# Weights in two longer rings, with a distance within 512 bytes for each kind of product

## What is computed

```python
def first_block(x, ...):          # DEPTH = 2
    for layer in range(DEPTH):
        y = rms_norm(h, nw[0])
        y = even_mixer(...) if layer % 2 == 0 else odd_mixer(...)   # attention + gated recurrence / attention with bias
        h = h + rms_norm(y, nw[1])
        y = conv_ffn(rms_norm(h, nw[2]), ffn_w_up[layer], ...)      # 1024 -> 2 x 2816, conv, 2816 -> 1024
        h = h + rms_norm(y, nw[3])

def second_block(x, mem, ...):    # one layer
    proj = rms_norm_2(x, g_mix) @ w_in      # q, k, v of three attentions, three gates
    merged = sum of sigmoid(gate) * (attention @ w_br)
    x = x + merged @ w_out
    x = x + (silu(h2 @ w_gate) * (h2 @ w_up)) @ w_down
```

## Time and profile before

| what | us |
|---|---|
| median of 3 runs | 1095.84 |
| lowest, highest | 1094.64, 1097.82 |
| profiled execution | 1095.88 |
| span in its profile | 1094.1 |
| PE busy | 1086.6 |
| DVE busy | 748.6 |
| ACT busy | 600.4 |
| POOL busy | 109.1 |

### The profile page before, as it was taken

One profiled execution on the slowest core, in us unless ns is written; L12 is line 12 of the kernel. 1 busy time (PEld: TensorE's weight loads), 2 busy tenths in 40 slices (PEclk: granted clock), 3 DMA queues, 4 the chain that ended last, 5 costly groups with the idle time before them and its releaser, 6 DMA issues.

```text
span 1094.1 us, 16723 instructions
## 1 busy us (share of the span) xinstructions
PE 1086.6 (99%) x6712; PEld 959.6 (88%) x6712; DVE 748.6 (68%) x1109; ACT 600.4 (55%) x994; POOL 109.1 (10%) x127
## 2 busy tenths in 40 slices
PE   8999999999999999999999999999999999999998
PEld 7988989888888899898888888889999989888887
DVE  7876595998846566859788566766656885666651
ACT  6744465776734545557667445357444644555640
POOL 4020000121100000001111001121000000111100
PEclk9999999999999999999999999999999999999999
DMA  8751356666664755366566656474433555666661
GB/s 287 284 174 59 121 206 211 193 190 188 185 192 152 269 150 146 126 225 189 187 190 184 195 182 212 135 234 135 115 99 113 167 159 196 189 181 187 192 193 39
DMA packets 56957, 192.29 MB, mean 176 GB/s; under 512 B 6832, under 2 KB 9776, under 8 KB 56880
## 3 DMA queue, kind: packets, MB, share of 16 engines
q1 hardware_dynamic: 56880, 191.22, 55.2%
HBM read 190.15 MB, written 1.05 MB: 175 GB/s over the span
## 4 chain that ended last, share of the span: by engine, by line
PE 95%; DVE 2%; POOL 1%; ACT 1%; issue 0%; DMA 0%; DVEq 0%; ACTq 0%; POOLq 0%
PE ps L929 28%; PE ps L1019 19%; PE ps L1010 15%; PE ps L1020 10%; PE ps L1285 5%; PE ps L1159 3%; PE ps L1105 3%; PE ps L1082 2%; PE ps L1346 2%; PE ps L1094 1%; PE ps L1031 1%; PE ps L1144 1%; DVE lo L1485 1%; POOL hr L533 1%; PE ps L1051 1%; PE ps L1169 1%
## 5 line engine op out<-in xcount | busy, mean ns | idle before, releaser
L1485 DVE TENSOR_TENSOR lo<-raw,hi 128x1024 fp32r<-128x1024 f32 (+2 forms) x347 | 429.1, 1263 | 81.9 <-ACT hi L588 79.1
L588 ACT ACTIVATE hi<-raw 128x1024 fp32r<-128x1024 f32 (+2 forms) x347 | 347.0, 1036 | 82.2 <-DMA raw<-in_weights 75.5
L1019 PE MATMUL ps<-y_both,hi 128*128 128x512 f32 x912 | 320.8, 397 | 0.0
L1020 PE MATMUL ps<-y_both,lo 128*128 128x256 f32 x912 | 255.0, 280 | 0.0
L1019 PEld LDWEIGHTS ps<-y_both,hi 128*128 128x128 f32 x912 | 171.3, 188 | 41.5
L1020 PEld LDWEIGHTS ps<-y_both,lo 128*128 128x128 f32 x912 | 171.9, 189 | 0.0
L1010 PE MATMUL ps<-y_both,hi 128*128 128x256 f32 x912 | 167.6, 285 | 0.3 <-DVE lo L1485 0.3
L1010 PEld LDWEIGHTS ps<-y_both,hi 128*128 128x128 f32 x912 | 141.8, 191 | 1.1 <-DVE lo L1485 0.5
L1010 PE MATMUL ps<-y_both,lo 128*128 128x256 f32 x456 | 128.9, 283 | 0.0
L929 PE MATMUL ps<-hi,y_both 128*128 128x512 f32 x352 | 94.1, 382 | 2.2 <-DVE lo L1485 1.4
L929 PE MATMUL ps<-hi,h_hi 128*128 128x512 f32 x294 | 90.9, 391 | 0.0
(11 more groups left out here) (291 smaller groups left out, 1386.2 us busy)
## 6 DMA issues: line engine op xcount, KB each, us to landing
raw<-in_weights SPq DMA_DIRECT2D x331, 512.0 KB, 3.7
gain<-in_gains SPq DMA_DIRECT2D x10, 512.0 KB, 7.2
raw<-in_weights SPq DMA_DIRECT2D x8, 384.0 KB, 7.2
bias<-in_rel SPq DMA_DIRECT2D x16, 128.0 KB, 2.1
raw<-in_weights SPq DMA_DIRECT2D x8, 256.0 KB, 2.6
mem_x<-in_mem SPq DMA_DIRECT2D x2, 512.0 KB, 9.8
h<-in_x SPq DMA_DIRECT2D x2, 256.0 KB, 2.7
h<-in_x SPq DMA_DIRECT2D x1, 512.0 KB, 6.1
```

Source lines behind the costliest of these rows:

```text
L588: act.activation(hi[:, s, :w], raw[:, s, :w], ACT.Copy).then_inc(hi_done, 1)
L1019: pe.matmul(dst, hi[:, s, at], y_both[:, :, k, :], start=k == 0, stop=False)
L1020: mm = pe.matmul(dst[:, 0:S], lo[:, s, at], y_hi[:, k, :], start=False, stop=k == KD - 1)
L1485: dve.tensor_tensor(lo[:, s, :w], raw[:, s, :w], hi[:, s, :w].bitcast(F32), ALU.subtract).then_inc(lo_done, 1)
```

## The change

The slots are replaced by two rings of single values. `lo` and `raw` get LO_RING = 10 x 1024 + 144 values, `hi` gets HI_RING = 10 x 1024 + 240. DIST gives for a kind two distances in steps of 64 bytes, of hi and of lo: how far, modulo 512 bytes, token slices lie behind weight slices. Feature-major kinds get (1, 7), leads and up get (1, 0), all others (0, 0). `ring()` places each unit in each ring behind the one before, moved up to the next place that has its distance, or at the front where the ring's end is reached; GIVER is the latest unit that lay on any part of either place. The load's semaphore goes by n modulo 10. To make room, block_causal moves into mk_t, snk and esnk into top and tot, warm is cut, and align goes. The places at the changes of kind, worked out from the code: units 8 to 14 and 16 to 22 have a giver 7 before them instead of 8; units 32 and 33 start in or reach into the kept region and have giver 31; units 34 to 39 have one 10 before them; 40 has giver 31 as before, 41 has 32 instead of 31 and 42 has 33 instead of 32; 84 to 92, 114 to 122, 130 to 132, 134 to 142, 182, 184 to 190, 237 to 242, 244, 245, 274 to 282 and 325 to 332 have one 9 before them instead of 10; all others keep 10.

```diff
+DIST = {"even_f": (1, 7), "even_q": (1, 7), "odd_qk": (1, 7), "gates": (1, 7), "branches": (1, 7),
+        "lead0": (1, 0), "lead1": (1, 0), "lead2": (1, 0), "up0": (1, 0), "up1": (1, 0), "up2": (1, 0)}
+STEP, LINE = 16, 128
+LO_RING, HI_RING = RAW * UNIT + LINE + STEP, RAW * UNIT + LINE + 7 * STEP
 def ring():
-    free = [(s, -1) for s in range(FEW)]
+    kept = (RAW - FEW) * UNIT
+    names = [name for name, n, _, _ in STREAM for _ in range(n)]
+    owner = [[-1] * HI_RING, [-1] * LO_RING]
+    end, at, giver = [0, 0], [], []
     for n in range(UNITS):
-        free.append((free[n][0], n))
-        if n == last("fill") - 1:
-            free += [(s, n) for s in range(FEW, RAW)]
-    slot, giver = [x[0] for x in free[:UNITS]], [x[1] for x in free[:UNITS]]
-    return slot, giver, [slot[:n + 1].count(slot[n]) for n in range(UNITS)]
+        both, last_owner = [], -1
+        for i, size in enumerate((HI_RING, LO_RING)):
+            if n < last("fill"):
+                size -= kept
+            elif n == last("fill"):
+                owner[i][size - kept:] = [n - 1] * kept
+            rest = STEP * ((7, 0)[i] - DIST.get(names[n], (0, 0))[i]) % LINE
+            p = end[i] + (rest - end[i]) % LINE
+            if p + UNIT > size:
+                p = rest
+            end[i] = p + UNIT
+            last_owner = max(last_owner, *owner[i][p:p + UNIT])
+            owner[i][p:p + UNIT] = [n] * UNIT
+            both.append(p)
+        at.append(both)
+        giver.append(last_owner)
+    return at, giver
...
-            lo = sb("lo", [RAW, UNIT], F32R, r)
-        raw = sb("raw", [RAW, UNIT])
-        hi = sb("hi", [RAW, UNIT], F32R)
+            lo = sb("lo", [LO_RING], F32R, r)
+        raw = sb("raw", [LO_RING])
+        hi = sb("hi", [HI_RING], F32R)
...
-        m_hi = lo[:, FEW:RAW, :].rearrange("p a (b s) -> p (a b) s", s=S)
-        m_lo = hi[:, FEW:RAW, :].rearrange("p a (b s) -> p (a b) s", s=S)
+        m_hi = lo[:, LO_RING - (RAW - FEW) * UNIT:].rearrange("p (k s) -> p k s", s=S)
+        m_lo = hi[:, HI_RING - (RAW - FEW) * UNIT:].rearrange("p (k s) -> p k s", s=S)
...
-                sp.dma_start(raw[:, SLOT[n], :WIDTH[n]], dram["weights"][n][:, :WIDTH[n]]).then_inc(raw_in[SLOT[n]], 16)
+                sp.dma_start(raw_at(n)[:, :WIDTH[n]], dram["weights"][n][:, :WIDTH[n]]).then_inc(raw_in[n % RAW], 16)
```

More of the change, by code:

```diff
@@ L227, in build @@
         mv = sb("mv", [NT, 512])
+        block_causal = mk_t[:, 0, 0:P].bitcast(U32)
         sc = sb("sc", [2, 512])
@@ L254, in build @@
         rec = sb("rec", [20, 2])
-        snk = sb("snk", [8, 2])
-        esnk = sb("esnk", [8, 2])
+        snk, esnk = top[:, 8:16, :], tot[:, 8:16, :]
         ncum = sb("ncum", [S])
@@ L471, in _ @@
                 (keep[:, :], dram["c_keep"]),
[L472 removed]
+                (window[:, :], dram["c_window"]), (block_causal, dram["c_block"]),
                 (hw[:, :], dram["hgrn_w"].partition_broadcast(P)),
@@ L778, in _ @@
                     act.activation(whole(hg), whole(hg), ACT.Silu).then_inc(hg_evac, 1)
-                    act.activation(warm[:, 8:16], half[:, 8:16], ACT.Exp)
+                    act.activation(warm[:, :], half[:, 8:16], ACT.Exp)
                 if hh in (4, 6):
@@ L785, in _ @@
             act.wait_ge(dve_sink, 1)
-            act.activation(esnk[:, :, :], snk[:, :, :], ACT.Exp).then_inc(act_sink, 1)
+            act.activation(esnk, snk, ACT.Exp).then_inc(act_sink, 1)
             even_hi(1, 1, 2)
@@ L888, in _ @@
             gate_copy(11)
-            act.activation(warm[:, 8:16], half[:, 8:16], ACT.Sigmoid)
+            act.activation(warm[:, :], half[:, 8:16], ACT.Sigmoid)
             for b in range(4):
@@ L1008, in features_of @@
                         at = slice(k * cols + f * P, k * cols + (f + 1) * P)
-                        for w, x, first, final in ((hi, yh, True, False), (hi, yl, False, False), (lo, yh, False, True)):
-                            mm = pe.matmul(dst, w[:, s, at], x(k), start=first and k == 0, stop=final and k == nk - 1)
+                        for w, x, first, final in ((hi_at, yh, True, False), (hi_at, yl, False, False), (lo_at, yh, False, True)):
+                            mm = pe.matmul(dst, w(n)[:, at], x(k), start=first and k == 0, stop=final and k == nk - 1)
                 return mm
             def features_pair(n, dst):
-                s = SLOT[n]
                 pe.wait_ge(lo_done, n + 1)
@@ L1018, in features_pair @@
                     at = slice(k * P, (k + 1) * P)
-                    pe.matmul(dst, hi[:, s, at], y_both[:, :, k, :], start=k == 0, stop=False)
-                    mm = pe.matmul(dst[:, 0:S], lo[:, s, at], y_hi[:, k, :], start=False, stop=k == KD - 1)
+                    pe.matmul(dst, hi_at(n)[:, at], y_both[:, :, k, :], start=k == 0, stop=False)
+                    mm = pe.matmul(dst[:, 0:S], lo_at(n)[:, at], y_hi[:, k, :], start=False, stop=k == KD - 1)
                 return mm
@@ L1142, in _ @@
                         k = 2 * (n - FIRST["even_i"]) + kk
-                        for x, w in ((y_hi, hi), (y_hi, lo), (y_lo, hi)):
-                            mm = pe.matmul(ps[:, 4 + t, :], x[:, k, t * P:(t + 1) * P], w[:, SLOT[n], 512 * kk:512 * kk + 512],
-                                           start=k == 0 and x is y_hi and w is hi, stop=k == KD - 1 and x is y_lo)
+                        for x, w in ((y_hi, hi_at), (y_hi, lo_at), (y_lo, hi_at)):
+                            mm = pe.matmul(ps[:, 4 + t, :], x[:, k, t * P:(t + 1) * P], w(n)[:, 512 * kk:512 * kk + 512],
+                                           start=k == 0 and x is y_hi and w is hi_at, stop=k == KD - 1 and x is y_lo)
                 mm.then_inc(unit_used, 1)
@@ L1157, in fill @@
                         wait_unit(n)
-                    for x, w in ((yh, hi), (yh, lo), (yl, hi)):
-                        mm = pe.matmul(ps[:, 6, t * 256:t * 256 + 256], x[:, k, t * P:(t + 1) * P], w[:, SLOT[n], c],
-                                       start=k == 0 and x is yh and w is hi, stop=k == KD - 1 and x is yl)
+                    for x, w in ((yh, hi_at), (yh, lo_at), (yl, hi_at)):
+                        mm = pe.matmul(ps[:, 6, t * 256:t * 256 + 256], x[:, k, t * P:(t + 1) * P], w(n)[:, c],
+                                       start=k == 0 and x is yh and w is hi_at, stop=k == KD - 1 and x is yl)
                     if t == 1 and k % 4 == 3:
@@ L1189, in even_part @@
                     wait_unit(n)
-                for x, w in ((y_hi, hi), (y_hi, lo), (y_lo, hi)):
+                for x, w in ((y_hi, hi_at), (y_hi, lo_at), (y_lo, hi_at)):
                     for c in range(2):
-                        mm = pe.matmul(ps[:, (0, 6)[t] + c, :], x[:, k, tok], w[:, SLOT[n], 512 * c:512 * c + 512],
-                                       start=u == 0 and x is y_hi and w is hi, stop=u == KD - 1 and x is y_lo)
+                        mm = pe.matmul(ps[:, (0, 6)[t] + c, :], x[:, k, tok], w(n)[:, 512 * c:512 * c + 512],
+                                       start=u == 0 and x is y_hi and w is hi_at, stop=u == KD - 1 and x is y_lo)
                 if t == 1:
@@ L1284, in lead @@
                                     k, c = 4 * half_ + kk, slice(256 * kk, 256 * kk + 256)
-                                    mm = pe.matmul(lead_place(layer, j, t), x[:, k, tok], w[:, SLOT[n], c],
+                                    mm = pe.matmul(lead_place(layer, j, t), x[:, k, tok], w(n)[:, c],
                                                    start=k == 0 and i == 0, stop=k == KD - 1 and i == 2)
@@ L1343, in out_part @@
                     wait_unit(n)
-                for x, w in ((0, hi), (0, lo), (1, hi)):
+                for x, w in ((0, hi_at), (0, lo_at), (1, hi_at)):
                     for c in range(2):
-                        mm = pe.matmul(ps[:, (6, 0)[t] + c, :], out_y(x, k // 4, tok)[:, k % 4, :], w[:, SLOT[n], 512 * c:512 * c + 512],
-                                       start=k == 0 and x == 0 and w is hi, stop=k == KD - 1 and x == 1)
+                        mm = pe.matmul(ps[:, (6, 0)[t] + c, :], out_y(x, k // 4, tok)[:, k % 4, :], w(n)[:, 512 * c:512 * c + 512],
+                                       start=k == 0 and x == 0 and w is hi_at, stop=k == KD - 1 and x == 1)
                 if t == 1:
```

55 lines of the change are left out of this document (30 added, 25 removed).

## The result

| what | before | after |
|---|---|---|
| median, runs timed together | 1096.83 us (1094.64 to 1098.11) | 1117.1 us (1116.52 to 1118.75) |
| span of the profiled execution | 1094.1 us | 1115.8 us |
| mean granted TensorE clock | 1.00 | 0.988 |

The changed kernel is slower by 1.9%: the ratio is 1.0187, with a 95% interval of 1.0169 to 1.0205. It is 20.3 us longer, where 8.9 us were predicted. The direction and the range held, and the size was half of what came. In the changed kernel the same lines have numbers higher by 28 or 29: L929 is now L958, L1010 is L1039, L1019 and L1020 are L1047 and L1048, L1285 is L1313, L1031 is L1059, L1192 is L1220, L1346 is L1374.

What follows compares the result with a forecast made beforehand. PE, busy for 99% of the span, was taken as the bound. 1095.9 us less 23.7 saved by quicker products plus 32.6 for waits and restarts gave 1104.8 us, range 1083 to 1128.

Steps and rivals of the forecast that it cites:

- The four stops: New PE waits around even_out and odd_out because loads get later givers: 28.6 us of cost, bounds 27 and 30.
- A: Going into even_out, units 32 and 33 wait for unit 31: PE idles 7.3 to 9.1 us, 8.3 taken.
- B: Leaving even_out, unit 42 waits for unit 33 and holds up the norms: 7.1 us of new PE wait.
- C: In odd_out, unit 139 waits for 130 and its hi holds up out_hi: PE waits 5.9 us at out_part(4, 0).
- D: Leaving odd_out, unit 140 waits for 131, the first of the second pass: 7.3 us of PE wait.
- the waits are covered after all: Rival: engines not held up by unit order, or quicker loads, leave about 10 us of cost: 1082 us, chance 0.08.
- Starting again: Behind each of four idle spells PE runs at half pace: 0 to 9.6 us of cost, 4 taken.
- Feature-major products: 1440 products in even_f, even_q, odd_qk, gates and branches go from 120 to 112 ns: 11.4 us saved.
- Pairs: 912 pairs of 512 and 256 columns in the up stages go to 339 ns each: 10.0 us saved.
- The start: At the kernel's start units 8 to 14 come one release later: costs nothing, 1.5 us at most.
- The distance takes all of it away: Rival: feature-major and lead products reach 109 ns, pairs 325: 43.4 us saved, 1085 us, chance 0.20.
- The distance does nothing: Rival: the excess is a fixed cost of switching weights, so nothing is saved: 1128.5 us, chance 0.17.

Runs made afterwards that it cites:

- e1: The kernel before, slots and addresses kept, but each load waits for the later of its own giver and the changed kernel's: 1133.65 us, ratio 1.0328.
- e2: The changed kernel, but the ring may use the kept region only from unit 40 on: 1099.41 us, ratio 1.0021.
- e3: e2 with odd_qk, even_out and odd_out also at distance (1, 0), so the rings don't shift between them: 1083.39 us, ratio 0.9872.
- e8: The changed kernel with an empty DIST table, so new rings without distances: 1106.23 us, ratio 1.0079.
- e4: A kernel of its own, writing zeros, that sweeps 8 x 8 distances for feature-major products and pairs; products timed start to start, no kernel time given.
- e7: e3 with (3, 1) for even_f, even_q, gates and branches alone, the other kinds left at (1, 0): 1079.92 us, ratio 0.9844.
- e6: e3 with (3, 1) in place of (1, 7) and (3, 0) in place of (1, 0): 1090.04 us, ratio 0.9931.
- e5: A kernel of its own like e4, writing zeros, that sweeps the distances for token-major products of 512 columns and leads; no kernel time given.

## Why the prediction was right and where it was wrong

The four waits came where they were forecast and for the reason given, and the kernel became slower; the loss was more than twice the 8.9 us of the sum. Two terms of the sum carry that: the feature-major products, taken at 11.4 us of saving, gave 3.3, and starting again, taken at 4 us of cost, took 8.5.

- **The four stops: right.** 28.6 us were taken, with bounds of 27 and 30; 26.4 came in after and 27.0 in e1. A was put at 8.3 us and took 7.1; B 7.1 and 6.9; C 5.9 and 5.5; D 7.3 and 6.9. The part of A that was put too high is the landing: the first load of the queue took about 3.6 us with loads behind it, so the lower of the two ends held. e1 shows the releases as their cause by themselves, e2 and e3 take them away by placing alone. The rival "the waits are covered after all" fell.
- **Starting again: the mechanism was right, the term was mis-sized by half.** The text read half pace for 4.8 us at the kernel's start, 2.4 us a time, set a bound of 9.6 for four, and then took 4, "as part of it falls where PE then waits for DVE anyway". That was an argument without a row. The stops measured 1.8, 2.3, 2.5 and 1.9 us, 8.5 in all, and e8's single one 2.1. Nothing was hidden: behind each stop PE has products that wait for nobody, and the distance to the kernel before doesn't shrink afterwards. The granted clock, which showed nothing at the kernel's start, does show it here (0.50 from 139.90 to 146.40). The Trainium skill, "TensorE: Matmul & The Clock Gate", section "What's actually happening", has an idle TensorE fall to 1.2 GHz and back to 2.4 GHz only after being busy again, and under "Wait — 56ns, not 53.3ns?" gives starts exactly N/1.2 GHz apart until then; the 427 ns for 512 columns agree with it. The stops of 5.5 us and more brought it; the 1.4 us one did not.
- **Feature-major products: the term that failed.** 11.4 us were taken, 3.3 came. The step was "I take 112 ns, the quick half of the pairs". The quick pace does exist and was close, 113.3 ns; what was wrong is that the step took it for all 1440 products. It assumed without a word that one distance has one pace. At (1, 7) there are two, 113.3 and 118.9, and most gates and all of branches ran at the slower one; odd_qk's later units, in trains of 24 products between other work, lie at 117 to 124 ns there, against 123 before. With (3, 1), which holds the quick pace however it is entered (e4), the gain over e3 is 3.5 us in time, to a total of 1079.92 us (e7).
- **Pairs: right.** 10.0 us taken, 9.8 came (320.5 to 310.7, where the prediction had 319.2 to 309.2), 340 ns against 339. e6 shows that this was partly luck: at (3, 0) they would have given nothing.
- **Leads: half.** 2.3 taken, 1.1 came; they run at 117 to 118 ns on average, not at 112 for two thirds of them.
- **The start: the number fell within its bound by luck.** "Nothing, 1.5 us at most" was 1.3, but not for the reason given. PE waits for no late load there; it waits for a y_lo that DVE makes beside POOL, before any load with a new giver is issued.
- **The rivals.** "The distance takes all of it away" (109 ns) fell in e4: no distance reaches it. "The distance does nothing" fell in e1 against after, 1133.65 against 1117.1 us with the same stops. The Trainium skill's statement in "TensorE: Matmul & The Clock Gate", section "Step-by-step: what each phase is for", that loading the next weights takes no read bandwidth from the running matmul, doesn't fit either, if no address could change a product's time by it: 120.0 ns went to 113.4 in e7. Where in the chip load and stream meet, no run here shows.

From 8.9 us predicted to what the spans show: features 8.1 us less saved, restart 4.5 more, leads and pairs 1.4 less saved, the start (DVE beside POOL) 1.3 more, the stops 2.2 less, and the old wait at B 0.3 less. That is 8.9 + 8.1 + 4.5 + 1.4 + 1.3 - 2.2 - 0.3 = 21.7 us.

What stays open is what picks the pace in which a train of products is caught. The sweep, and after beside e2, say that it hangs on how the train is entered, and e6 that (3, 0) and (1, 0) part ways in the kernel; no rule for it came out.

## What to carry to other kernels

A new placing in a ring changes who releases whom, so walk the givers unit by unit and look for engines that take units in a fixed order ahead of work that PE waits for: a release one unit later cost nothing in most places and 5.5 to 7 us in three, and one six or seven units later cost 7 us. A stop of PE of that length costs itself and then about 2 us of half clock; count both in full. And where matmuls of this type follow each other with a weight load each, the distance of the two operands' addresses is worth a try, kind by kind and measured in the kernel itself, since a distance can have two paces.

## What the runs showed of the hardware

- A product of fp32r with 256 columns starts 120 ns after the one before at distance 0 modulo 256 bytes, and down to 113 ns at other distances; a pair of 512 and 256 columns takes 347 to 353 or 340 ns; a 512-column product with tokens held still is quickest at distance 0 (227 ns, 228 to 234 elsewhere). The pattern repeats after 256 bytes, exactly or nearly (e4, e5).
- One distance can have two steady paces, 113.3 ns (the four units of even_f in after) and 118.9 (240 products of branches in after). One longer distance between two products can leave the pace as it was (217 ns once, in after) or change it (160 ns once, in e2).
- Behind 5.5 to 7.2 us without work, PE ran products of 512 columns 427 ns apart, for 3.2 to 5.6 us in all eleven stops (four in after, four in e1, two in e2, one in e8), at a cost of 1.5 to 2.5 us each. The granted clock read 0.50 already before the stop was over.
- DVE's 128x512 `y_both<-pt,y_both` took 0.69 us alone and 1.6 to 1.8 us when POOL's `xhat<-mem_x,gain` had begun before it (after, e1, e3, e6, e7; in e2 the first took 1.19).
